# Final normalisation stage: nine in-place row buffers, loads issued by SyncE and ScalarE, stores by GpSimd and SyncE

## The chip, the cores and the metric

One Trainium2 chip, one of its cores. The time is device time of one execution in microseconds; a smaller number is better. The engines are TensorE (PE), VectorE (DVE), ScalarE (ACT), GpSimd (POOL) and SyncE (SP). Transfers between the chip's memory (DRAM) and its on-chip buffer (SBUF) run on 16 DMA engines; they are issued from SyncE's, ScalarE's or GpSimd's instruction stream, each into a queue of its own.

## What is computed

One layer of a trunk: modulation, a token mixing part with a convolution and a recurrent branch, then an expert-choice mixture of sixteen experts, for 1024 latent rows and 128 context rows of 1024 values each. The change concerns the last step alone, the final RMSNorm of both row sets:

```
def rmsnorm(x, g):
    xf = x.astype(jnp.float32)
    y = xf * lax.rsqrt(jnp.mean(xf * xf, axis=-1, keepdims=True) + EPS)
    return (y * g.astype(jnp.float32)).astype(x.dtype)
...
    xp, S_ctx = trunk_layer(xp, c_ctx, s_zero, T_p, *shared)
    xs, _ = trunk_layer(xs, c, state_hgrn[:, l], GRID_W, *shared)
    y_prompt = rmsnorm(xp, final_norm)
    y_sample = rmsnorm(xs, final_norm)
```

## The kernel before

The kernel is written with hand-placed semaphores. It runs in stages. Between two stages stands a barrier of all engines, so that no instruction of a stage is issued before all engines have left the one before it. The last but one stage is the experts': its results are added by indirect transfers from GpSimd into the tensor `x1_d` in DRAM, 1152 rows (nine tiles of 128 rows by 1024 float32, 512 KB each; tiles 0 to 7 are the latent rows, tile 8 the context rows). The last stage reads the nine tiles back, normalises them and stores them as outputs. TensorE has no work in it.

In the last stage:

- SyncE issues the load of `FN` (the row `final_norm`, broadcast to 128 partitions, L2152), then the nine loads `XF <- x1_d` (L2156). `XF` has four buffers: from tile 4 on each load waits until VectorE has finished with tile t - 4, by the semaphore `f_out`.
- ScalarE takes the tiles in order: a Square with a row sum (L2164, in the trace with a short instruction that reads the sum), a Ln (L2167) and an Exp (L2170) make the factor 1 / sqrt(mean + EPS) in `RS3`.
- VectorE multiplies the tile by this factor and by `FN` (L2180) into `YF`, which has three buffers: from tile 3 on it waits for the store of tile t - 3 (`y_stored`).
- GpSimd waits for each result and issues its store (L2187), and at the end waits for all nine.

What sets the order is the order of the tiles in each of the four instruction streams, and the two pools of buffers. The names in the trace leave numbers out: `x_d` is `x1_d`, `out_dram` the output tensors, `RS` is `RS3`, `XJ` the unused squares.

Of the kernel before, what the change touches and what calls it, by code (L numbers as in the profile page):

```python
# [8 lines left out]
ACT = mybir.ActivationFunctionType  # L9
# [7 lines left out]
P = 128  # L17
D = 1024
KT = D // P
TL = 8  # L20
TN = TL + 1
# [55 lines left out]
def trunk(nc, x_prompt, x_sample, state, cond, c_ctx, w_ada, b_ada, norm1, w_in, conv_w, conv_b,  # L77
# [3 lines left out]
    with ctx:  # L81
# [6 lines left out]
        def sem(name):  # L88
            stage_sems.append(nc.alloc_semaphore(name))
            return stage_sems[-1]  # L90
# [7 lines left out]
        def scratch(name, shape):  # L98
            return nc.dram_tensor(name, shape, F32, kind="Internal").ap()
# [7 lines left out]
        x1_d = scratch("x1_d", [T, D])  # L107
# [99 lines left out]
        def wload(eng, slot, src, col):  # L207

            eng.dma_start(W_FULL[:, slot, 1], src[:, :, ds(col, P)]).then_inc(weights_in[slot], 16)
# [31 lines left out]
        with nc.Block() as block:  # L241
            @block.sync
            def _(sp):
                sp.dma_start(CR[0:1, :], c_ctx.rearrange("(a n) -> a n", a=1)).then_inc(cond_in, 16)
                sp.dma_start(CR[1:2, :], cond).then_inc(cond_in, 16)
                for d in range(2):
                    sp.dma_start(LBI[8 * d:8 * d + 8], hgrn_lb[d].rearrange("j (c f) -> c j f", f=P)) \
                      .then_inc(lbi_in, 16)
                sp.dma_start(CST[:], consts).then_inc(const_in, 16)
                for i in range(2):  # L250
                    sp.dma_start(AW[:, i], w_ada_v[:, :, i * 512:(i + 1) * 512]).then_inc(ada_in[i], 16)
                sp.dma_start(MODR[:], b_ada[0].partition_broadcast(2)).then_inc(rows_in, 16)
                sp.dma_start(NR[:, 0, :], norm1[0].partition_broadcast(2)).then_inc(rows_in, 16)
                sp.dma_start(NR[:, 1, :], norm2[0].partition_broadcast(2)).then_inc(rows_in, 16)
                for b in range(2, ADA):

                    sp.wait_ge(ada_mm, b - 1)
                    sp.dma_start(AW[:, b % 2], w_ada_v[:, :, b * 512:(b + 1) * 512]).then_inc(ada_in[b % 2], 16)
                    if b == 9:

                        sp.wait_ge(cond_ct, 1)
                        for slot, off in enumerate((ZF, ZB, IV)):
                            wload(sp, slot, w_in_v, off)
                for slot, off in ((3, Q), (4, OG)):
                    wload(sp, slot, w_in_v, off)
                sp.wait_ge(mod_out, 48)
# [1866 lines left out]

        fn = Region(nc, after_w, hi)
        FN = fn("FN", [P, D])
        XF = fn("XF", [P, 4, D])
        YF = fn("YF", [P, 3, D])
        XJ3 = fn("XJ3", [P, D])
        RS3 = fn("RS3", [P, 2, TN])
        fn_in = sem("fn_in")  # L2140
        xf_in = [sem(f"xf_in{i}") for i in range(4)]
        f_sq = sem("f_sq")
        f_ln = sem("f_ln")
        f_rs = sem("f_rs")
        f_out = sem("f_out")
        y_stored = [sem(f"y_stored{i}") for i in range(3)]
        y_rows = [y_sample[0, t * P:(t + 1) * P, :] for t in range(TL)] + [y_prompt[0]]

        with nc.Block() as block:
            @block.sync  # L2150
            def _(sp):
                sp.dma_start(FN[:], final_norm.partition_broadcast(P)).then_inc(fn_in, 16)  # L2152
                for t in range(TN):
                    if t >= 4:
                        sp.wait_ge(f_out, t - 3)
                    sp.dma_start(XF[:, t % 4], x1_d[t * P:(t + 1) * P, :]).then_inc(xf_in[t % 4], 16)  # L2156

            @block.scalar
            def _(act):
                for t in range(TN):  # L2160
                    act.wait_ge(xf_in[t % 4], 16 * (t // 4 + 1))
                    if t:
                        act.wait_ge(f_sq, t)
                    nc.scalar.activation(XJ3[:], XF[:, t % 4], ACT.Square,  # L2164
                                         accum_out=RS3[:, 0, t:t + 1]).then_inc(f_sq, 1)
                    act.wait_ge(f_sq, t + 1)
                    nc.scalar.activation(RS3[:, 0, t:t + 1], RS3[:, 0, t:t + 1], ACT.Ln, bias=EPS,  # L2167
                                         scale=1.0 / D).then_inc(f_ln, 1)
                    act.wait_ge(f_ln, t + 1)
                    nc.scalar.activation(RS3[:, 1, t:t + 1], RS3[:, 0, t:t + 1], ACT.Exp,  # L2170
                                         scale=-0.5).then_inc(f_rs, 1)

            @block.vector
            def _(dve):
                dve.wait_ge(fn_in, 16)
                for t in range(TN):
                    dve.wait_ge(f_rs, t + 1)
                    if t >= 3:
                        dve.wait_ge(y_stored[t % 3], 16 * (t // 3))  # L2179
                    nc.vector.scalar_tensor_tensor(YF[:, t % 3], XF[:, t % 4], RS3[:, 1, t:t + 1], FN[:],  # L2180
                                                   ALU.mult, ALU.mult).then_inc(f_out, 1)

            @block.gpsimd
            def _(pool):
                for t in range(TN):
                    pool.wait_ge(f_out, t + 1)
                    pool.dma_start(y_rows[t], YF[:, t % 3]).then_inc(y_stored[t % 3], 16)  # L2187
                for i in range(3):
                    pool.wait_ge(y_stored[i], 48)


# [24 lines left out]
```

## Time and profile before

| | us |
|---|---|
| median of 3 runs | 2624.31 |
| lowest and highest | 2623.44, 2630.18 |
| the profiled execution, its own time | 2623.36 |
| its span | 2621.6 |
| last stage, first issue to end of the span | 2587.36 to 2621.6 |
| TensorE busy over the span | 2430.2 (93%) |
| VectorE busy | 1024.7 (39%) |
| ScalarE busy | 841.9 (32%) |
| GpSimd busy | 368.8 (14%) |

The span is what the profiler saw of the execution, from its first to its last event; the execution's own time is a little longer. The shares are averages over all stages, and most of the span is matrix work; the last stage, some 34 us at its end, is read from its own window. Issuing a transfer isn't counted as busy time of an engine; a "q" behind an engine's name means its instruction queue.

### The profile page before, as it was taken

What the parts mean: (1) busy time and instruction counts of PE and PEld (TensorE: products, weight loads), DVE (VectorE), ACT (ScalarE), POOL (GpSimd) and SP (SyncE); (2) the same over time, 40 slices, a digit from 0 to 9 for tenths busy, and PEclk for the clock granted to TensorE, in tenths of its full rate; (3) what the DMA queues carried; (4) which work ended last, traced back from release to release, by engine and by line L of the source; (5) the groups of instructions that cost most, each with busy time, mean ns of one, the idle gap of its engine ahead of it and who ended that gap; (6) DMA issues with size and microseconds to landing.
All of it is one profiled execution on the core that took longest, in us unless ns stands there. A gap on an engine that the chain in (4) does not pass through costs nothing. (4 is left out here: it accounts for less than half of the span.)

```text
span 2621.6 us, 47354 instructions
## 1 busy us (share of the span) xinstructions
PE 2430.2 (93%) x17645; PEld 2293.1 (87%) x17645; DVE 1024.7 (39%) x2630; ACT 841.9 (32%) x1989; POOL 368.8 (14%) x611
## 2 busy tenths in 40 slices
PE   7799999999999999999979989749999999999992
PEld 2399999999999999999979988549999999999992
DVE  2455364545446363545522434642122222222222
ACT  2454444444454444445422012101112111211112
POOL 0011110202111021111111114201010011101011
PEclk9899999999999999999989999879999999999996
DMA  7512112021211112121163433738887887788754
GB/s 268 173 43 62 51 51 62 27 80 35 77 35 55 59 43 72 30 77 43 60 217 101 133 104 121 264 106 267 292 265 242 275 292 253 239 290 283 242 187 161
DMA packets 368217, 376.22 MB, mean 144 GB/s; under 512 B 11803, under 2 KB 340539, under 8 KB 368096
## 3 DMA queue, kind: packets, MB, share of 16 engines
q1 hardware_dynamic: 353928, 326.58, 37.1%
q0 software_dynamic: 14160, 47.81, 6.6%
q8 instruction: 102, 1.67, 0.3%
q14 instruction: 17, 0.14, 0.0%
q10 hardware_dynamic: 10, 0.02, 0.0%
HBM read 330.82 MB, written 43.55 MB: 143 GB/s over the span
## 5 line engine op out<-in xcount | busy, mean ns | idle before, releaser
L717 PE MATMUL bank<-HT,W 128*128 128x384 f32 x5760 | 1049.3, 338 | 27.8 <-issue 15.7
L717 PEld LDWEIGHTS bank<-HT,W 128*128 128x128 f32 x5760 | 995.6, 188 | 33.1 <-issue 30.1
L2016 PE MATMUL bank<-XET,WEA 128*128 128x144 f32 x4096 | 510.9, 287 | 0.6 <-DVE XET L2088 0.6
L2016 PEld LDWEIGHTS bank<-XET,WEA 128*128 128x128 f32 x4096 | 505.5, 191 | 1.3 <-issue 0.7
L2031 PE MATMUL bank<-HID,WED 128*128 128x144 f32 x2048 | 257.8, 287 | 0.0
L2031 PEld LDWEIGHTS bank<-HID,WED 128*128 128x128 f32 x2048 | 252.6, 190 | 0.7
L1409 PE MATMUL bank<-YO,W 128*128 128x384 f32 x960 | 172.0, 336 | 18.5 <-ACT YO L1425 18.5
L1409 PEld LDWEIGHTS bank<-YO,W 128*128 128x128 f32 x960 | 168.3, 189 | 18.8 <-issue 18.8
L2047 ACT ACTIVATE SG<-bank 128x144 f32<-128x144 f32 x128 | 37.3, 291 | 409.5 <-PE bank L2016 409.5
L2117 DVE TENSOR_TENSOR GU<-SG,bank 128x144 f32<-128x144 f32 x128 | 38.9, 304 | 300.4 <-ACT SG L2051 300.4
L2055 ACT ACTIVATE YT<-bank 128x144 f32<-128x144 f32 x128 | 37.3, 291 | 274.3 <-PE bank L2031 274.3
L2099 DVE SCALAR_TENSOR_TENSOR YS<-bank,TW,G 128x512 f32<-128x512 f32 x32 | 24.0, 751 | 254.8 <-PE bank L1993 254.8
L1046 DVE TENSOR_TENSOR W<-W_FULL,W 128x1024 fp32r<-128x1024 f32 x80 | 98.6, 1232 | 32.5 <-ACT W L853 32.4
L1294 POOL TENSOR_TENSOR KH<-X 128x256 f32<-128x256 f32 x32 | 26.4, 835 | 574.2 <-DVE X L1061 387.5
L1935 POOL DMA_INDIRECT x_d<-YS,IDX x16 | 31.3, 1959 | 408.4 <-DVE YC L2099 408.4
L1053 DVE TENSOR_SCALAR KK<-ZS,CWP 128x384 f32<-128x384 f32 x48 | 23.0, 480 | 166.5 <-ACT ZS L868 166.5
L853 ACT ACTIVATE W<-W_FULL 128x1024 fp32r<-128x1024 f32 x80 | 83.7, 1046 | 0.0
L325 PE MATMUL bank<-AW,CT 128*2 128x512 f32 x160 | 73.9, 619 | 6.7 <-DMA AW<-in_w_ada_dram 6.6
L1161 DVE TENSOR_SCALAR ON<-bank,RST 128x128 f32<-128x128 f32 x72 | 25.2, 350 | 128.8 <-ACT RST L980 128.8
L623 POOL TENSOR_TENSOR G<-X 128x128 f32<-128x128 f32 x72 | 35.6, 495 | 270.5 <-PE bank L767 270.5
L2123 DVE TENSOR_TENSOR HID<-GU,bank 128x144 f32<-128x144 f32 x128 | 39.0, 304 | 88.7 <-PE bank L2016 88.7
L949 ACT ACTIVATE QR<-bank 128x384 f32<-128x384 f32 x48 | 23.6, 492 | 143.9 <-PE bank L717 143.9
(218 smaller groups left out, 2794.3 us busy)
## 6 DMA issues: line engine op xcount, KB each, us to landing
WEA<-in_w_e_gate_dram SPq DMA_DIRECT2D x64, 1024.0 KB, 4.8
WEA<-in_w_e_up_dram SPq DMA_DIRECT2D x64, 1024.0 KB, 10.5
WED<-in_w_e_down_dram SPq DMA_DIRECT2D x64, 1024.0 KB, 9.7
W_FULL<-in_w_in_dram SPq DMA_DIRECT2D x80, 512.0 KB, 3.7
AW<-in_w_ada_dram SPq DMA_DIRECT2D x10, 2048.0 KB, 9.0
sg_d<-QR SPq DMA_DIRECT2D x48, 192.0 KB, 1.9
GL<-sg_d POOLq DMA_DIRECT2D x48, 192.0 KB, 2.7
ya_d<-CY SPq DMA_DIRECT2D x24, 192.0 KB, 1.9
```

The lines of the kernel that those rows point to most:

```text
L325: ins = nc.tensor.matmul(PS[1 + b % 2][0:2, :], CT[:, k, :], AW[:, b % 2, k, :], start=(k == 0), stop=(k == KT - 1))
L623: vec.tensor_tensor(o, a, b, ALU.subtract)
L717: ins = nc.tensor.matmul(bank[:, 0:CH], W[:, slot, a, k, :], HT[:, b, k, at * CH:(at + 1) * CH], start=(i == 0 and k == 0), stop=(i == 2 a ...
L853: nc.scalar.activation(W[:, slot, 0], W_FULL[:, slot, 1], ACT.Copy).then_inc(w_hi, 1)
L1046: nc.vector.tensor_tensor(W[:, slot, 1], W_FULL[:, slot, 1], W[:, slot, 0].bitcast(F32), ALU.subtract).then_inc(w_lo, 1)
L1409: ins = nc.tensor.matmul(PS[j % 4][:, 0:CH], W[:, m, a, k, :], src[:, k, n * CH:(n + 1) * CH], start=(i == 0 and k == 0), stop=(i == 2 and ...
L2016: ins = nc.tensor.matmul(PS[2 * s + f % 2][:, 0:NX], WEA[:, 4 * s + f // 2, k, (f % 2) * P:(f % 2 + 1) * P], XET[:, k, :], start=(k == 0), ...
L2031: ins = nc.tensor.matmul(PS[f % 4][:, 0:NX], WED[:, f // 2, k, (f % 2) * P:(f % 2 + 1) * P], HID[:, k, :], start=(k == 0), stop=(k == KT - 1))
L2047: nc.scalar.activation(b, PS[f % 2][:, 0:NX], ACT.Exp, scale=-1.0).then_inc(g_exp, 1)
L2055: nc.scalar.activation(YT[:, f // 4, f % 4], PS[f % 4][:, 0:NX], ACT.Copy).then_inc(yt_made, 1)
L2117: nc.vector.tensor_tensor(GU[:, f % 2], SG[:, f % 2], PS[f % 2][:, 0:NX], ALU.mult) \
L2123: nc.vector.tensor_tensor(HID[:, f], GU[:, f % 2], PS[2 + f % 2][:, 0:NX], ALU.mult) \
```

## The change

The last stage gets a buffer for each of the nine tiles, and VectorE writes its result over the tile that it reads, so that `YF` is gone and no load or result waits for a buffer. The loads are shared: SyncE issues FN and then tiles 1, 3, 5 and 7, ScalarE issues tiles 0, 2, 4, 6 and 8 ahead of its first computation. The stores are shared too: GpSimd issues those of the even tiles, SyncE those of the odd ones, behind its loads. Each load has a semaphore of its own, each storing engine one semaphore for its stores.

```
-        XF = fn("XF", [P, 4, D])
-        YF = fn("YF", [P, 3, D])
+        XF = fn("XF", [P, TN, D])
...
                 sp.dma_start(FN[:], final_norm.partition_broadcast(P)).then_inc(fn_in, 16)
-                for t in range(TN):
-                    if t >= 4:
-                        sp.wait_ge(f_out, t - 3)
-                    sp.dma_start(XF[:, t % 4], x1_d[t * P:(t + 1) * P, :]).then_inc(xf_in[t % 4], 16)
+                for t in range(1, TN, 2):
+                    sp.dma_start(XF[:, t], x1_d[t * P:(t + 1) * P, :]).then_inc(xf_in[t], 16)
+                for t in range(1, TN, 2):
+                    sp.wait_ge(f_out, t + 1)
+                    sp.dma_start(y_rows[t], XF[:, t]).then_inc(y_stored[1], 16)
+                sp.wait_ge(y_stored[1], 64)
...
             @block.scalar
             def _(act):
+                for t in range(0, TN, 2):
+                    act.dma_start(XF[:, t], x1_d[t * P:(t + 1) * P, :]).then_inc(xf_in[t], 16)
                 for t in range(TN):
-                    act.wait_ge(xf_in[t % 4], 16 * (t // 4 + 1))
+                    act.wait_ge(xf_in[t], 16)
...
                     dve.wait_ge(f_rs, t + 1)
-                    if t >= 3:
-                        dve.wait_ge(y_stored[t % 3], 16 * (t // 3))
-                    nc.vector.scalar_tensor_tensor(YF[:, t % 3], XF[:, t % 4], RS3[:, 1, t:t + 1], FN[:],
+                    nc.vector.scalar_tensor_tensor(XF[:, t], XF[:, t], RS3[:, 1, t:t + 1], FN[:],
                                                    ALU.mult, ALU.mult).then_inc(f_out, 1)
...
-                for t in range(TN):
+                for t in range(0, TN, 2):
                     pool.wait_ge(f_out, t + 1)
-                    pool.dma_start(y_rows[t], YF[:, t % 3]).then_inc(y_stored[t % 3], 16)
-                for i in range(3):
-                    pool.wait_ge(y_stored[i], 48)
+                    pool.dma_start(y_rows[t], XF[:, t]).then_inc(y_stored[0], 16)
+                pool.wait_ge(y_stored[0], 80)
```

SyncE's instructions at the end of the program, as a difference (the branches are the ends and beginnings of the stages' code; x9 stands for nine of a kind):

```order
 L1908 COMPARE_AND_BRANCH
 L1901 UNCONDITIONAL_BRANCH
-L2150 UNCONDITIONAL_BRANCH
-L2152 DMA FN<-in_final_norm_dram 128x1024
-L2156 DMA XF<-x_d 128x1024 x9
 L2149 UNCONDITIONAL_BRANCH
+L2151 DMA FN<-in_final_norm_dram 128x1024
+L2153 DMA XF<-x_d 128x1024 x4
+L2156 DMA out_dram<-XF 128x1024 x4
+L2148 UNCONDITIONAL_BRANCH
```

Five of nine loads have left SyncE's stream, and four stores have come in behind the rest.

ScalarE's instructions at the start of the last stage in the changed kernel, up to the end of its first tile:

```order
 L2041 COMPARE_AND_BRANCH
 L1901 UNCONDITIONAL_BRANCH
...
+L2159 UNCONDITIONAL_BRANCH
+L2162 DMA XF<-x_d 128x1024 x5
+L2167 ACTIVATE XJ_7168,RS_7169<-XF 128x1024
+L2170 ACTIVATE RS_7169<-RS_7169 128x1
+L2173 ACTIVATE RS_7169<-RS_7169 128x1
```

The five issues stand ahead of the first tile's three computations; those and all later ones are as before.

GpSimd's instructions at the end of the program, as a difference:

```order
 L1901 UNCONDITIONAL_BRANCH
 L94 ISA
-L2183 UNCONDITIONAL_BRANCH
-L2187 DMA out_dram<-YF 128x1024 x9
-L2149 UNCONDITIONAL_BRANCH
+L2184 UNCONDITIONAL_BRANCH
+L2188 DMA out_dram<-XF 128x1024 x5
+L2148 UNCONDITIONAL_BRANCH
```

Four of nine stores have left GpSimd's stream.

## Rows read from the trace of the kernel before

**Rows 1.** Chain that ended last, 2587 us on: start us, us, what.

```profile
2587.76 5.54 DMA XF<-x_d
...
2598.08 8.01 DMA out_dram<-YF
...
2606.18 1.29 DVE YF L2180
...
2607.49 6.67 DMA XF<-x_d
...
2617.41 0.53 POOL out_dram L2187
```

**Rows 2.** Waits of the last stage: total us, times, longest us.

```profile
ACT XJ L2164 <- DMA XF<-x_d: 30.6, 6, 22.3
DVE YF L2180 <- DMA out_dram<-YF: 9.9, 4, 3.1
...
SPq L2156 <- DVE YF L2180: 16.4, 5, 6.6
```

**Rows 3.** Stretches: length, PE, PEld, DVE, ACT, POOL busy, PEclk, DMA share, GB/s.

```profile
2588.50:2620.00 31.50, 0.00 (x0) 0.00 (x0) 11.56 (x9) 13.66 (x36) 4.91 (x9) 0.50 0.86 317
2588.50:2591.00 2.50, 0.00 (x0) 0.00 (x0) 0.00 (x0) 0.00 (x0) 0.00 (x0) 0.50 0.60 221
2591.00:2595.50 4.50, 0.00 (x0) 0.00 (x0) 0.45 (x1) 2.11 (x5) 0.00 (x0) 0.50 1.02 414
2595.50:2597.00 1.50, 0.00 (x0) 0.00 (x0) 1.35 (x2) 1.44 (x5) 0.35 (x1) 0.50 0.34 137
2597.00:2599.00 2.00, 0.00 (x0) 0.00 (x0) 1.78 (x2) 1.93 (x6) 0.84 (x2) 0.50 0.86 129
2599.00:2603.50 4.50, 0.00 (x0) 0.00 (x0) 1.56 (x2) 2.00 (x7) 0.53 (x1) 0.50 0.96 369
2603.50:2608.50 5.00, 0.00 (x0) 0.00 (x0) 2.19 (x2) 3.06 (x8) 1.06 (x2) 0.50 1.03 419
2608.50:2611.00 2.50, 0.00 (x0) 0.00 (x0) 1.30 (x2) 1.55 (x4) 0.53 (x1) 0.50 0.96 200
2611.00:2614.50 3.50, 0.00 (x0) 0.00 (x0) 0.43 (x2) 0.32 (x1) 0.53 (x1) 0.50 0.99 404
2614.50:2617.00 2.50, 0.00 (x0) 0.00 (x0) 2.38 (x2) 1.24 (x4) 0.53 (x1) 0.50 0.37 151
2617.00:2620.00 3.00, 0.00 (x0) 0.00 (x0) 0.12 (x1) 0.00 (x0) 0.53 (x1) 0.50 0.85 350
2620.00:2621.60 1.60, 0.00 (x0) 0.00 (x0) 0.00 (x0) 0.00 (x0) 0.00 (x0) 0.50 0.00 0
...
2592.00:2592.50 0.50, 0.00 (x0) 0.00 (x0) 0.00 (x0) 0.00 (x0) 0.00 (x0) 0.50 1.06 434
```

**Rows 4.** DMA queues, 2587 us on: packets, MB, share of 16 engines.

```profile
q1 hardware_dynamic: 1440, 5.24, 45.0%
q0 software_dynamic: 1296, 4.72, 33.3%
```

**Rows 5.** Timeline: the first issue of the last stage.

```profile
2587.36 0.35 SPq L2152 DMA_DIRECT2D FN<-in_final_norm_dram  x1
```

**Rows 6.** Timeline: first and fourth tile on ScalarE; groups by line: VectorE's.

```profile
2593.33 1.06 ACT L2164 ACTIVATE XJ<-XF 128x1024 f32<-128x1024 f32 x1 [22.31 <-DMA XF<-x_d]
...
2597.86 1.04 ACT L2164 ACTIVATE XJ<-XF 128x1024 f32<-128x1024 f32 x1
...
L2180 DVE SCALAR_TENSOR_TENSOR YF<-XF,RS,FN 128x1024 f32<-128x1024 f32 x9 | 11.6, 1284 | 32.3 <-ACT RS L2170 22.0 <-DMA out_dram<-YF 9.9
```

**Rows 7.** Timeline of the first stage: two issues by ScalarE, one by SyncE.

```profile
0.90 0.56 ACTq L271 DMA_DIRECT2D CWR<-in_conv_w_dram  x1
1.49 0.23 ACTq L272 DMA_DIRECT2D CWR<-in_conv_b_dram  x1
...
4.18 5.12 SPq L252 DMA_DIRECT2D MODR<-in_b_ada_dram  x1
```

## What the change should do to the time

> **What bounds the kernel now.** The edit touches only the last stage, so I first asked where that stage begins and what ends it. The chain of waits over its window [rows 1] shows no matrix work: from 2587.76 us it runs from a load of 5.54 us through ScalarE and VectorE into a store of 8.01 us, from there through one VectorE operation of 1.29 us into a load of 6.67 us, and from that load through ScalarE and VectorE to the last store. Three transfers take 20.2 of the 33.8 us. The two joints are buffers: VectorE may not write tile 4 until the store of tile 1 has emptied its YF buffer, and SyncE may not load tile 8 until VectorE has finished with an XF buffer. The list of waits says the same in totals: VectorE stood 9.9 us behind stores, SyncE's queue 16.4 us behind VectorE, ScalarE 30.6 us behind loads, of which 22.3 are the start of the stage [rows 2].
>
> Next I asked whether the transfers are slow by themselves. The stretches of the stage [rows 3] give the bytes per second in each. The whole, 2588.5 to 2620.0, moves 31.5 x 317 = 9.99 MB, and the two queues say 5.24 + 4.72 = 9.96 MB [rows 4]. Where both queues have work in hand (2603.5 to 2608.5) the rate is 419 GB/s. At that rate the bytes need 23.8 us, so 31.5 - 23.8 = 7.7 us are lost somewhere. Each stretch loses its length times (1 - rate / 419): 1.2 us in 2588.5 to 2591, 0.05 in the next, 1.0 in 2595.5 to 2597, 1.4 in 2597 to 2599, 0.5 in 2599 to 2603.5, nothing in the next, 1.3 in 2608.5 to 2611, 0.1, then 1.6 in 2614.5 to 2617 and 0.5 in 2617 to 2620; together 7.7. Behind the last byte stand 1.6 us in which nothing moves [rows 3], and before the first 1.1 us from the issue at 2587.36 [rows 5]. Both stay.
>
> **What the engines need.** ScalarE takes a tile every (2597.86 - 2593.33) / 3 = 1.51 us when its loads are there, VectorE 1.28 us [rows 6]. Nine tiles are 13.6 us on ScalarE and 1.3 more on VectorE for the last. From a start at 2593.33, which is where the first load let it begin, VectorE would be done at 2608.2, and the last store would be issued 0.3 later. That is before the 2588.5 + 23.8 = 2612.3 at which the transfers can be through at best. So with buffers for all tiles the stage is bound by its bytes, and my sum is about which of the 7.7 us of lost transfer time come back.
>
> **The change part by part.** The loads: nine buffers instead of four, so none of the five waits in SyncE's queue is left, and every load is in a queue within the first 2 us. *The gap 2595.5 to 2599* (2.4 us) was a queue that had run dry after four tiles, and then a load that started anew. With nine loads in hand the dry part, 1.0 us, surely goes. The slow restart, 1.4 us at 129 GB/s, goes too if it is a restart, and stays if it is the reading of that tile. I take that it goes, since the first four tiles ran at 414 GB/s from the same tensor behind one another: 2.4 back, at the least 1.0.
>
> *The stretch 2608.5 to 2611* (1.3 us at 200 GB/s) is less clear: tile 8 had been asked for at 2607.49 [rows 1], and stores were in hand too, yet the rate fell by half. Either it is again a load started behind a drained queue (gone now) or reads and stores getting in each other's way (it stays or grows). Bounds 0 and 1.3, and I take the middle, 0.65. The 0.5 and 0.1 us of the mixed stretches I leave lost.
>
> *The tail.* From 2614.5 the transfers ran dry because tile 8's load had only just landed: ScalarE, VectorE and the store's issue follow it in series [rows 1]. In the changed kernel, tile 8 leaves VectorE near 2608.2, and then some 1.7 MB of stores are still to be moved (4.1 us at 419), so its own latency is covered. 1.6 + 0.5 = 2.1 us come back, as long as the load of tile 8 has landed in time. From its landing to the end there were 2621.6 - 2614.16 = 7.4 us; for the end that I forecast, 2621.6 - 5.75 = 2615.85, it has to land by 2608.4. Until the first store can move (some 2597) the loads have 8.5 us, which is 3.0 MB of their 5.24 if FN stays slow and 3.5 if not. If they get half of the rate while stores share it, the other 1.7 to 2.2 MB take 8 to 10.5 us (2605 to 2607.5); with two of three queues' shares, 6 to 8 us (2603 to 2605). So it should be in time, with little room, and at the low end I let 0.5 of the 2.1 be lost.
>
> *ScalarE issues five loads.* Its other issues in this program took 0.56 and 0.23 us [rows 7]; five by these are 1.2 to 2.8 us, from about 2587.4 to 2590.2 at the latest, and it has nothing to do before 2592. They lie under the first load, cost 0. Even an issue that is held up, as SyncE's of 5.12 us in the first stage [rows 7], would end by 2593. What this buys: tile 0 is no longer behind FN in one queue. The stretch 2588.5 to 2591 is FN, one row read 128 times, at 221 GB/s, that is 1.2 us lost. If tile 0's packets fill the holes, up to 1.2 come back; if the broadcast holds up the engines themselves, nothing. No row shows two load queues, so I take half, 0.6.
>
> A rule of the Trainium skill speaks against this piece: "DMA: Bandwidth & Descriptors", section "Rules for kernel authors", says that spreading transfers over SyncE, ScalarE and GpSimd brings no bandwidth, since all share the same 16 engines, and saves only issue time. By it the 0.6 are 0 and the gain is 5.15 in place of 5.75. The trace bears it out as far as it goes: one queue alone runs at 414 GB/s, two at 419 [rows 3].
>
> *The stores.* Five by GpSimd (0.53 us an issue [rows 1]) and four by SyncE; three waits of VectorE and the buffers behind them go, 9.9 us of VectorE's idle time in all, but only the parts counted above are on the path. SyncE's stores of tiles 1, 3, 5, 7 stand in its queue behind its own loads of tiles 1 to 7 and wait for VectorE; nothing else is issued behind them. The issue time of a store is hidden as long as stores are in backlog. No bytes are added or taken away; writing in place takes the same three operands of VectorE, cost 0.
>
> **The sum.** 2.4 + 0.65 + 2.1 + 0.6 = 5.75 us. The profiled run took 2623.36 us, 1.76 of it outside its span, and would be 2617.6; the median of the runs shown is 0.95 above that run, so the forecast is 2624.31 - 5.75 = **2618.6 us**, 0.22% less. At the low end 1.0 + 0 + 1.6 + 0 = 2.6 us come back (2621.7), at the high end all 7.7 (2616.6).
>
> The same page's specifications give about 358 GB/s for HBM per core. By that figure, as an estimate, the bytes need 27.9 us and the stage gains 3.6. The trace differs: 419 GB/s over 5 us [rows 3].
>
> **The rivals.** (1) *Reads stay slow beside stores, the gain is small.* For it: the stretch 2608.5 to 2611, and 369 GB/s in 2599 to 2603.5. Against: 419 in 2603.5 to 2608.5 with the same mixture. Two such stretches more than I keep, 1.3 us each, and the slow restart of 1.4 us staying leave 5.75 - 2.6 - 1.4 = 1.75 us: 2622.6. (2) *Slower than before.* If every store that starts beside reads costs such a stretch, 1.3 us for each of nine, 11.7 are added to a best case of 7.7 gained: 4.0 slower, 2628.3. It decides from six stores on (6 x 1.3 = 7.8), and nothing shows it for more than two of the nine. (3) *Everything comes back and the rate is above 419*, since two load queues and two store queues leave no hole: the bytes at 434 GB/s, which one half microsecond reached [rows 3], need 22.9 us, 8.6 gained, 2615.7. Against: no longer stretch is above 419. (4) *The change doesn't do what it says*: if the nine loads can't all be in hand because a queue holds up the issue, as for 5.12 us in the first stage [rows 7], the loads still arrive at the rate of the transfers, and it costs at most the dry 1.0: 2619.6, hardly to be told from the forecast.
>
> **How the numbers follow.** Forecast with its bounds, 2616.5 to 2621.7, and rival 4 with it: 0.72. Rival 1, 2621.7 to 2625: 0.10. Rival 3, gains over 7.9 us: 0.13. Slower than 2625, rival 2 in whole or in part: 0.05, of which 0.03 over 0.3%. A change of 0.3%, 7.9 us, is about the least that a measurement of this kernel can tell from none. So faster by more than that is 0.13, slower 0.03, and 0.84 lie within. The range leaves out half of rival 3 and the far side of rivals 1 and 2: 2615.7 to 2623.5.
>
> **What would show it.** In the changed kernel's profile: the last byte moves near 2614 and the span ends near 2615.8; the rate from 2589 to the end has no stretch under 300 GB/s but the first; VectorE waits for no store; VectorE's last operation ends before 2610, with four stores still on the way. If tile 8's load lands after 2607, the tail has come back. If the stretch of the first 2.5 us stays at 221 GB/s, the 0.6 are gone. The forecast is wrong if the rate falls to 200 whenever stores and loads mix, or if the time moves by more than 8 us, since then something besides this stage's transfers has changed.

## The result, and the profile after

The changed kernel takes 2619.8 us in the median of 20 runs, the kernel before 2624.4 in the median of 20: a ratio of 0.9982 with a 95% interval of 0.9975 to 0.9989, that is 4.6 us less, between 2.9 and 6.6. The forecast was 2618.6 us, 5.75 us less, inside a range of 2615.7 to 2623.5. The interval leaves out a ratio of 1, so the kernel is faster, but by less than the 0.3% that the prediction took as the least that can be told well from none; a change inside that bound was thought most likely.

The last stage, where all of the edit is, shows more than the whole does. Its length, from the first issue to the end of the span, fell from 34.24 us (2587.36 to 2621.6) to 28.03 us. The timeline of the changed kernel at the start of the stage and at its end (start us, us, engine, line, operation):

```profile
2586.57 0.35 SPq L2151 DMA_DIRECT2D FN<-in_final_norm_dram  x1
2586.59 2.89 ACTq L2162 DMA_DIRECT2D XF<-x_d  x5
2586.98 2.26 SPq L2153 DMA_DIRECT2D XF<-x_d  x4
2592.22 1.06 ACT L2167 ACTIVATE XJ<-XF 128x1024 f32<-128x1024 f32 x1 [21.76 <-DMA XF<-x_d]
...
2606.78 1.28 DVE L2181 SCALAR_TENSOR_TENSOR XF<-XF,RS,FN 128x1024 f32<-128x1024 f32 x1 [0.23 <-ACT RS L2173]
2608.35 0.53 POOL L2188 DMA_DIRECT2D out_dram<-XF  x1 [2.48 <-DVE XF L2181]
```

All nine loads are issued within 2.9 us. VectorE's last operation ends at 2608.1, and the span at 2614.6, so the stage runs on for 6.5 us behind it, with stores in all but its last 1.6 us; before, VectorE ended at 2617.1 and the end came 4.5 us later. The waits of the stage in the changed kernel (total us, times, longest), to be held against [rows 2]:

```profile
POOL out_dram L2188 <- DVE XF L2181: 29.3, 5, 18.8
DVE XF L2181 <- ACT RS L2173: 23.8, 9, 21.3
ACT XJ L2167 <- DMA XF<-x_d: 22.5, 2, 21.8
```

VectorE waits for no store any more (9.9 us before), and ScalarE waits for a load twice in place of six times, both at the start. The stretches of the changed kernel (length, busy time of PE, PEld, DVE, ACT, POOL, granted clock, share of the DMA engines, GB/s), which answer to [rows 3]:

```profile
2587.50:2613.00 25.50, 0.00 (x0) 0.00 (x0) 11.56 (x9) 13.23 (x36) 2.79 (x5) 0.50 1.01 391
2587.50:2591.00 3.50, 0.00 (x0) 0.00 (x0) 0.00 (x0) 0.00 (x0) 0.00 (x0) 0.50 0.96 256
2591.00:2596.50 5.50, 0.00 (x0) 0.00 (x0) 1.57 (x2) 3.43 (x9) 0.62 (x1) 0.50 1.01 413
2596.50:2599.00 2.50, 0.00 (x0) 0.00 (x0) 2.28 (x2) 2.38 (x8) 0.00 (x0) 0.50 1.02 419
2599.00:2601.00 2.00, 0.00 (x0) 0.00 (x0) 1.55 (x3) 1.94 (x6) 0.57 (x1) 0.50 1.02 397
2601.00:2612.50 11.50, 0.00 (x0) 0.00 (x0) 6.16 (x5) 5.49 (x16) 1.59 (x3) 0.50 1.03 420
2613.00:2614.60 1.60, 0.00 (x0) 0.00 (x0) 0.00 (x0) 0.00 (x0) 0.00 (x0) 0.50 0.01 3
```

The same 9.97 MB go in 25.5 us instead of 31.5. Against 419 GB/s 1.7 us are lost (25.5 x (1 - 391 / 419)) where 7.7 were, and 1.4 of them lie in one place, the first 3.5 us (3.5 x (1 - 256 / 419)). From there to 2612.5, half a microsecond before the last byte, the engines run at 397 to 420 GB/s.

Why does the whole gain less than the stage? The experiments had both kernels traced a second time. The stage took 34.08 and 28.22 us there, so the pairs agree within 0.2 us, and the change is worth 34.16 - 28.12 = 6.0 us in it. That lies inside the interval of the whole, near its upper end. What scatters is the part ahead of the stage, which is the same code in both kernels. The first 300 us of the kernel before, of its second trace and of run e7 below:

```profile
0.00:300.00 300.00, 265.73 (x1539) 200.19 (x1540) 133.96 (x324) 128.78 (x277) 38.04 (x84) 0.97 0.37 127
```

```profile
0.00:300.00 300.00, 264.49 (x1516) 198.88 (x1517) 129.82 (x314) 126.14 (x272) 38.04 (x84) 0.95 0.38 126
```

```profile
0.00:300.00 300.00, 265.37 (x1498) 197.38 (x1499) 129.12 (x312) 123.53 (x266) 37.04 (x80) 0.94 0.37 125
```

The granted clock of TensorE there, a mean over the 300 us, is 0.97, 0.95 and 0.94, and in the same 300 us 1539, 1516 and 1498 matrix instructions are done. The last stage then begins at 2587.4, 2591.4 and 2596.6 us. This is several times the differences that are to be explained, and so the experiments are read by the length of the stage in their traces. The two traces of one kernel differed by 0.2 us in it. Each experiment below has a single trace, so a few tenths of a microsecond between two of them show nothing.

### The profile page after: what moved, and what is told of

It reads as the page before. It is cut to its first block and busy times, and to the rows that moved or that the text cites. A ratio compares the mean times of both kernels' runs of the same rounds, so it can differ in the third digit from the quotient of the medians.

```text
span 2614.6 us, 47348 instructions
## 1 busy us (share of the span) xinstructions
PE 2430.8 (93%) x17645; PEld 2293.9 (88%) x17645; DVE 1025.1 (39%) x2630; ACT 840.9 (32%) x1989; POOL 366.5 (14%) x607
## 6 DMA issues: line engine op xcount, KB each, us to landing
WEA<-in_w_e_up_dram SPq DMA_DIRECT2D x64, 1024.0 KB, 10.5
```

## The experiments

The stage's length in each trace (us from the first issue to the end of the span):

| kernel | stage |
|---|---|
| before, two traces | 34.24, 34.08 |
| the change, two traces | 28.03, 28.22 |
| e1: nine in-place buffers, loads by SyncE, stores by GpSimd | 28.90 |
| e2b: shared queues, four and three buffers | 31.95 |
| e3: nine load buffers, three result buffers | 30.92 |
| e4: four load buffers, nine result buffers | 31.86 |
| e5: before, tiles 4 to 8 read the rows of 0 to 3 and 0 | 33.61 |
| e6: the change, FN from 128 different rows | 27.99 |
| e7: the change, FN loaded in the experts' stage | 27.13 |
| e8: the change, loads by ScalarE, stores by SyncE | 27.97 |
| e10: e1 with FN loaded in the experts' stage | 27.43 |
| e11: the change, no store before the last loads | 29.81 |

The theory was that the nine buffers bring the gain, since they keep the transfer engines in work, and that the queues bring none. The rival was that the second load queue and the second store queue carry part of it.

### e1: the buffers alone

```
-                for t in range(1, TN, 2):
+                for t in range(TN):
                     sp.dma_start(XF[:, t], x1_d[t * P:(t + 1) * P, :]).then_inc(xf_in[t], 16)
...
-                for t in range(0, TN, 2):
-                    act.dma_start(XF[:, t], x1_d[t * P:(t + 1) * P, :]).then_inc(xf_in[t], 16)
...
-                for t in range(0, TN, 2):
+                for t in range(TN):
                     pool.wait_ge(f_out, t + 1)
                     pool.dma_start(y_rows[t], XF[:, t]).then_inc(y_stored[0], 16)
```

> The nine in-place buffers alone: all loads issued by SyncE, all stores by GpSimd, as before the change. The length of the last stage, from its first issue to the end of the span, was 34.2 us before and 28.0 with the whole change. Theory A (the buffers are the whole gain, all queues share the same engines): 27.8 to 28.8 us, ScalarE's first tile within 1 us of where it was, no stretch after the first 3 us under 380 GB/s. Theory B (the second load queue and the second store queue carry part of it): 29.5 us or more, with stretches under 350 GB/s after the first store.

Its stage took 28.90 us: 5.3 of the 6.0 us are there with one load queue and one store queue, just beyond the window of theory A and clear of theory B. The sign in the rates went the other way: theory A expected no stretch under 380 GB/s behind the start, and there is one under 350, as theory B had it. The whole kernel was at a ratio of 0.9968 (0.9957 to 0.998), 8.9 us less in the medians; 5.3 us is the edge of that interval, and the rest fits the scatter ahead of the stage (its trace enters the last stage at 2585.0 us, the earliest of all). The interval overlaps the change's (0.9975 to 0.9989), so this doesn't show that e1 beats the change; no measurement of the whole kernel shows either that the shared queues are worth having on top of the buffers. The stretches of e1 show most of what the last 0.8 us are:

```profile
2586.00:2589.50 3.50, 0.00 (x0) 0.00 (x0) 0.00 (x0) 0.00 (x0) 0.00 (x0) 0.50 0.97 282
2589.50:2595.50 6.00, 0.00 (x0) 0.00 (x0) 2.77 (x3) 4.69 (x13) 0.74 (x2) 0.50 1.02 416
2595.50:2598.00 2.50, 0.00 (x0) 0.00 (x0) 2.28 (x2) 2.40 (x7) 0.98 (x2) 0.50 0.99 320
2598.00:2611.50 13.50, 0.00 (x0) 0.00 (x0) 6.50 (x6) 6.13 (x18) 3.20 (x6) 0.50 1.01 414
```

One slow stretch, 320 GB/s for 2.5 us, costs 0.6 us; it begins 1.6 us after the first store's issue at 2593.94. All of the 0.80 MB that move in it belong to the load queue: the stores have been issued but move nothing yet. The changed kernel's only dip is 397 GB/s for 2 us, 0.1 us lost, 3.5 us after its first store's issue.

### e2b: the queues alone

```
+                def load(t):
+                    if t >= 4:
+                        sp.wait_ge(f_out, t - 3)
+                    sp.dma_start(XF[:, t % 4], x1_d[t * P:(t + 1) * P, :]).then_inc(xf_in[t % 4], 16)
+                load(1)
+                load(3)
+                for t in range(1, TN, 2):
+                    sp.wait_ge(f_out, t + 1)
+                    if t + 4 < TN:
+                        load(t + 4)
+                    sp.dma_start(y_rows[t], YF[:, t % 3]).then_inc(y_stored[t], 16)
...
+                load(0)
+                load(2)
                 for t in range(TN):
+                    if t in (2, 4, 6):
+                        load(t + 2)
```

> The queues alone: four load buffers and three result buffers as before, but even loads by ScalarE and odd ones by SyncE, even stores by GpSimd and odd ones by SyncE, each still waiting for its buffer. Theory A (the buffers are the gain): the waits stay, the stage keeps 33 to 35 us (before: 34.2), VectorE still waits about 10 us for stores. Theory B (the queues carry part of it): 32 us or less. Since SyncE's stores skip GpSimd's slow first store, some 1 us less than before is possible under A too.

31.95 us, 2.2 less than before: inside theory B's window, at its edge, and outside theory A's. So sharing the queues is worth something while buffers are short. In its trace the dry stretch and a slow one stand as before, but the one at tile 8 is gone:

```profile
2596.00:2598.00 2.00, 0.00 (x0) 0.00 (x0) 1.02 (x2) 1.70 (x5) 0.62 (x1) 0.50 0.19 78
2598.00:2600.00 2.00, 0.00 (x0) 0.00 (x0) 1.43 (x2) 1.94 (x5) 0.00 (x0) 0.50 1.00 344
2600.00:2603.00 3.00, 0.00 (x0) 0.00 (x0) 1.84 (x2) 2.18 (x8) 0.57 (x1) 0.50 1.03 268
2603.00:2614.00 11.00, 0.00 (x0) 0.00 (x0) 4.70 (x4) 6.28 (x17) 1.06 (x2) 0.50 1.02 410
```

VectorE waited 7.5 us for stores (9.9 and 10.3 in the two traces of before). A likely reading is that half of the stores no longer stand in line behind one another in one queue, so buffers come free a little sooner, and the loads that wait for them are issued sooner. It isn't shown: e2b shares the loads and the stores at once, and no run shares only one of them. The two parts alone gave 5.3 and 2.2 us, together 6.0: they mend the same losses, and with all buffers there the shared queues are left with 0.8 us. Even that isn't owed to two queues of each kind, since e8 below has one queue for all loads and one for all stores and is as short as the change (27.97 us).

### e3 and e4: which buffers

```
-        XF = fn("XF", [P, 4, D])
+        XF = fn("XF", [P, TN, D])
```

> Nine load buffers, three result buffers, loads by SyncE, stores by GpSimd. Theory A (a transfer queue that never runs dry is all that counts): VectorE still waits for stores, some 5 to 10 us in all, but the load queue is full until about 17 us into the stage and stores are in hand behind it, so the stage takes 28 to 29.5 us. Rival (VectorE's wait for stores is itself on the path): 31 us or more.

30.92 us, between the theory's 29.5 and the rival's 31, and close to the rival: VectorE's waits for stores are in part on the path. It waited 6.9 us for them, as thought, 5.7 at one time. The stores behind the loads did not stay in hand: from 2608 to 2618.5, with all reads done, the engines ran at 314 GB/s with at most three results on their way:

```profile
DVE YF L2178 <- DMA out_dram<-YF: 6.9, 3, 5.7
```

```profile
2602.50:2608.00 5.50, 0.00 (x0) 0.00 (x0) 1.28 (x1) 4.63 (x14) 0.00 (x0) 0.50 1.01 414
2608.00:2618.50 10.50, 0.00 (x0) 0.00 (x0) 6.38 (x5) 1.32 (x4) 3.20 (x6) 0.50 0.77 314
```

10.5 x (1 - 314 / 419) = 2.6 us are lost there. e1, which differs from e3 only in that results need no buffer of their own, is 2.0 us shorter. e4 has it the other way round:

```
-        YF = fn("YF", [P, 3, D])
+        YF = fn("YF", [P, TN, D])
...
-                    if t >= 3:
-                        dve.wait_ge(y_stored[t % 3], 16 * (t // 3))
```

> Four load buffers, nine result buffers, loads by SyncE, stores by GpSimd: VectorE never waits for a store, but loads from tile 4 on wait for VectorE. Theory A: the dry stretch after the first four tiles stays (1.0 us and 1.4 us of slow start), the rest runs near 400 GB/s: 30 to 31 us. Rival (the result buffers were the main brake): 28.5 us or less. Other rival (the load buffers were): 33 us or more.

31.86 us, beyond the theory's 31. The dry stretch and the slow one behind it are there, 2.0 us lost together (2.4 before), and then comes another 4.5 us at 328 GB/s (1.0 us) that I had not counted:

```profile
2595.50:2597.00 1.50, 0.00 (x0) 0.00 (x0) 1.35 (x2) 1.44 (x6) 0.62 (x1) 0.50 0.22 90
2597.00:2599.00 2.00, 0.00 (x0) 0.00 (x0) 1.74 (x2) 1.87 (x8) 0.57 (x1) 0.50 0.96 242
2599.00:2603.50 4.50, 0.00 (x0) 0.00 (x0) 2.57 (x2) 1.71 (x6) 1.41 (x3) 0.50 0.97 328
2603.50:2615.00 11.50, 0.00 (x0) 0.00 (x0) 5.14 (x4) 6.21 (x16) 1.78 (x4) 0.50 1.02 415
```

Against before (34.16 us, the mean of two traces) load buffers alone bring 3.2 us, result buffers alone 2.3, both 5.3 (e1, where result and load share a buffer). Neither pool was the brake by itself.

### e5: a new start, or a new place?

```
-                    sp.dma_start(XF[:, t % 4], x1_d[t * P:(t + 1) * P, :]).then_inc(xf_in[t % 4], 16)
+                    sp.dma_start(XF[:, t % 4], x1_d[(t % 4) * P:(t % 4 + 1) * P, :]).then_inc(xf_in[t % 4], 16)
```

> The kernel before, but the loads of tiles 4 to 8 read the rows of tiles 0 to 3 and 0 again (the outputs of tiles 4 to 8 are therefore not the reference's). It asks why the load after a pause ran at 129 GB/s (2 us) and tile 8's at 200 GB/s (2.5 us). Theory restart (it is the new start of a load behind a drained queue): both slow stretches stay, each costing 1 us or more, stage 33.5 to 35 us. Theory place (it is the reading of rows not touched for long, a new 2 MB piece at tile 4 and at tile 8): both go, stage 31 to 32.5 us.

33.61 us, and both slow stretches are there although from tile 4 on no load reads a row for the first time:

```profile
2596.00:2597.50 1.50, 0.00 (x0) 0.00 (x0) 1.35 (x2) 1.44 (x5) 0.42 (x1) 0.50 0.35 142
2597.50:2599.50 2.00, 0.00 (x0) 0.00 (x0) 1.78 (x2) 1.90 (x7) 0.77 (x2) 0.50 0.81 205
...
2609.50:2611.50 2.00, 0.00 (x0) 0.00 (x0) 1.73 (x2) 1.17 (x3) 0.15 (x1) 0.50 0.88 250
```

So the place of the rows isn't the cause. The stretches were somewhat milder (1.0 and 0.8 us lost, against 1.4 and 1.3), the second short of the 1 us that the theory asked for; one trace is no proof either way. A new start behind a drained queue fits both, and the changed kernel, which reads tiles 4 and 8 without a pause, shows neither. The start of the stage in e7 below, where FN isn't loaded and no store is issued yet, looks alike: the transfer engines are busy (share 1.03) and move little.

```profile
2597.50:2598.50 1.00, 0.00 (x0) 0.00 (x0) 0.00 (x0) 0.00 (x0) 0.00 (x0) 0.50 1.03 143
```

No run lets a drained queue start anew with nothing else changed, so this stays the reading that fits best.

### e6, e7 and e10: the slow first stretch

```
-                sp.dma_start(FN[:], final_norm.partition_broadcast(P)).then_inc(fn_in, 16)
+                sp.dma_start(FN[:], h2_d[0:P, :]).then_inc(fn_in, 16)
```

> The changed kernel, but FN is loaded from 128 different rows of the scratch tensor h2_d instead of one row 128 times (the outputs are therefore not the reference's). It asks what makes the first 3.5 us of the stage slow, 270 GB/s in place of 419. Theory broadcast (128 reads of one row hold up the engines): the first 3.5 us run at 380 GB/s or more, ScalarE starts 1 us or more earlier, and the stage takes 26.8 us or less (28.0 with the change). Theory start (the first reads of a stage are slow whatever they read): 250 to 300 GB/s as before and a stage of 27.7 to 28.3.

```profile
2590.50:2599.00 8.50, 0.00 (x0) 0.00 (x0) 2.66 (x3) 4.68 (x13) 0.62 (x1) 0.50 1.02 414
2599.00:2603.50 4.50, 0.00 (x0) 0.00 (x0) 3.83 (x4) 4.31 (x13) 0.57 (x1) 0.50 1.01 363
```

The start bears out the broadcast: with 128 different rows the transfers reach 414 GB/s from 2.1 us after the first issue on, where the change needs 4.4 us, and ScalarE begins at 5.0 us instead of 5.65 and 5.73 (0.7 earlier, where the theory asked for 1 or more). The end does not: the stage is 27.99 us, no shorter than the change's. What was won at the start is gone again in a stretch that begins 2.3 us after the first store, 4.5 us at 363 GB/s (0.6 us), six times the loss that the changed kernel had there. So the cost of FN's slow reading is real where it stands, but taking it away did not shorten the stage. It is also less than the 1.4 us lost in the change's first stretch: over the first 4.43 us from the first issue the change moves 202 and 203 GB/s in its two traces and e6 251, which is 0.22 MB, or 0.5 us at 419 GB/s. The rest is lost with 128 different rows too.

e7 issues FN's load in the experts' stage, into a place of its own at the end of the buffer memory:

```
+        FN = nc.alloc_sbuf_tensor_at("FN", [P, D], F32, offset=hi - D * 4)
...
                     sp.dma_start(G2[:, c], mod_d[c, 3].partition_broadcast(P)).then_inc(g2_in, 16)
+                sp.dma_start(FN[:], final_norm.partition_broadcast(P)).then_inc(fn_in, 16)
```

> The changed kernel, with FN loaded in the experts' stage into a place of its own, long before it is used. Both theories of the slow first stretch take away FN's 0.52 MB, 1.25 us at 419 GB/s. Theory broadcast: a further 1.2 us comes back, stage 25.3 to 25.9 us (28.0 with the change). Theory start: 26.5 to 27 us. The whole kernel should be 2 to 2.5 us or 1 to 1.5 us faster than the changed one, some 6.5 or 5.5 us faster than the kernel before.

27.13 us, 1.0 less than the change and above both windows, and e10, the same edit on e1, 27.43, 1.5 less than e1:

> FN loaded in the experts' stage, nine in-place buffers, all loads by SyncE and all stores by GpSimd. Beside the same with FN in the last stage (28.9 us) and beside FN earlier with shared queues (27.1 us). If the queues do nothing, this is 26.5 to 27.5 us, some 2 us less than with FN, of which 1.25 are its bytes; if the shared queues are worth the 0.8 us by which 28.9 and 28.1 differ, it is 27.7 to 28.2 us.

Both are about FN's bytes (1.25 us). e7 again has a slow stretch behind its first store:

```profile
2598.50:2606.50 8.00, 0.00 (x0) 0.00 (x0) 2.92 (x3) 4.82 (x13) 0.62 (x1) 0.50 1.01 414
2606.50:2610.00 3.50, 0.00 (x0) 0.00 (x0) 3.06 (x3) 3.37 (x10) 0.57 (x1) 0.50 0.95 301
```

e10's 27.43 lies in the window for "the queues do nothing", 0.3 us from e7. Its trace shows something that none of the theories has: one microsecond at 250 GB/s, from 4.0 us into the stage, 1.9 us before the first store is issued at 2598.87, with all nine loads in one queue and that queue alone at work.

```profile
2595.97:2596.97 1.00, 0.00 (x0) 0.00 (x0) 0.00 (x0) 0.94 (x4) 0.00 (x0) 0.50 0.96 250
```

A second slow stretch, 310 GB/s from 2600.5 to 2603, begins 1.6 us after the first store's issue, as in e1. As whole kernels e7 and the change are the same: on one chip and beside one another they took 2620.5 and 2620.6 us in the median of 12 runs each, both at a ratio of 0.998 (0.997 to 0.999 for e7, 0.9972 to 0.9989 for the change). The expectation for the change's second measurement:

> The changed kernel once more, beside the one above on the same chip, to see how much of the 6.2 us by which its last stage was shorter in the first trace is there again: stage 27.5 to 28.5 us, whole kernel 4.5 to 6.2 us faster than before. If the stage is again 6 us shorter and the whole only 4.5, something before the last stage costs 1 to 2 us or the runs scatter by as much.

4.6 us less than before, as in the first 20 runs, with a stage of 28.22 us. One more microsecond in the stage is below what this measurement shows, so the gain that was expected of e7 as a whole kernel, 1 us or more over the change, wasn't seen.

### e8 and e11: what makes transfers slow behind the first store

e8 takes GpSimd out of the stage: loads by ScalarE, FN and stores by SyncE.

```
-                for t in range(0, TN, 2):
+                for t in range(TN):
                     act.dma_start(XF[:, t], x1_d[t * P:(t + 1) * P, :]).then_inc(xf_in[t], 16)
...
-                for t in range(1, TN, 2):
+                for t in range(TN):
                     sp.wait_ge(f_out, t + 1)
                     sp.dma_start(y_rows[t], XF[:, t]).then_inc(y_stored[1], 16)
```

> The changed kernel with another split: all nine loads issued by ScalarE, FN and all nine stores by SyncE, none by GpSimd. In the runs so far reads fell to 250 to 340 GB/s for some 3 us, beginning 1 to 2 us after the first store was issued and before the first store's data moved, and GpSimd's first store took about 4 us from issue to its first data. Theory C (what GpSimd does for its first store of the stage disturbs the reads): no such stretch, all stretches after the first 3.5 us of the stage at 380 GB/s or more, a first store that moves data 1 us after its issue, stage 27.0 to 27.6 us. Theory D (writes to the output beside reads do it, whoever issues them): the stretch is there again, right with the first store's data, stage 27.8 to 28.8 us.

```profile
2594.38 13.76 SPq L2154 DMA_DIRECT2D out_dram<-XF  x9
```

```profile
2590.00:2597.00 7.00, 0.00 (x0) 0.00 (x0) 3.56 (x3) 5.47 (x14) 0.00 (x0) 0.50 1.02 414
2597.00:2599.00 2.00, 0.00 (x0) 0.00 (x0) 1.58 (x2) 1.87 (x8) 0.00 (x0) 0.50 1.01 322
2599.00:2612.00 13.00, 0.00 (x0) 0.00 (x0) 6.42 (x5) 5.99 (x16) 0.00 (x0) 0.50 1.02 419
```

The slow stretch is there, 2.6 us after SyncE's first store is issued, and the stage is 27.97 us. Theory C falls: the stretch comes without GpSimd, so GpSimd isn't needed for it. The stage is as short as the change's although all loads go through one queue and all stores through another. e1, 0.9 us longer, differs from e8 in three things: FN goes through the loads' queue, GpSimd issues the stores, and SyncE and not ScalarE issues the loads. No run tells which of them costs the 0.9 us. e11 holds all stores back until the loads of tiles 7 and 8 have landed:

```
+                sp.wait_ge(xf_in[TL - 1], 16)
+                sp.wait_ge(xf_in[TL], 16)
                 for t in range(1, TN, 2):
                     sp.wait_ge(f_out, t + 1)
...
+                pool.wait_ge(xf_in[TL - 1], 16)
+                pool.wait_ge(xf_in[TL], 16)
                 for t in range(0, TN, 2):
                     pool.wait_ge(f_out, t + 1)
```

> The changed kernel, but no store is issued before the loads of tiles 7 and 8 have landed, so that reads never meet a store. With stores in between, reads slowed down 2 to 3 us after the first store's issue, whoever issued it (GpSimd or SyncE), by 0.1 to 0.7 us in all. Theory D (the first stores beside reads do it): the loads run at 400 GB/s or more from 3.6 us after the stage's start to their end, some 15 us after it. Theory T (it comes at that time of the stage or in the middle of the loads, stores or not): a stretch under 370 GB/s at 10 to 14 us is there all the same. The stage itself should take 28 to 30 us, since the turn from loads to stores may leave the engines idle for 1 to 2 us.

```profile
2598.00:2608.00 10.00, 0.00 (x0) 0.00 (x0) 5.53 (x5) 7.86 (x21) 0.00 (x0) 0.50 1.02 417
2608.50:2609.50 1.00, 0.00 (x0) 0.00 (x0) 0.78 (x2) 0.94 (x5) 0.00 (x0) 0.50 0.01 4
```

With no store issued the loads run at 417 GB/s through the time at which the other kernels with nine buffers slow down, which is theory D against theory T: the slow stretch hangs on the first stores, and not on the time or the place in the loads. It needn't be their data, since in e1 they moved none while the rate was low. Nor is it the only thing that slows loads: e10 had its 250 GB/s before any store was issued. Keeping the two apart costs more than it saves, 29.81 us, most of it in the turn, where nothing moves for a microsecond. The cause of these dips stays open.

## Why the prediction held, point by point

- *The stage is bound by its bytes once every tile has a buffer*: right. Between 2591 and 2612.5 there is no stretch under 397 GB/s, and VectorE ends 6.5 us before the span.
- *The gap 2595.5 to 2599, 2.4 us*: all came back, and for the reason given as far as the runs show it. e4, which keeps four load buffers, keeps the gap; e5 shows that the slow part is not the reading of tile 4's rows. That it is the new start is what fits, not what a run shows by itself.
- *The stretch 2608.5 to 2611, half of 1.3 us*: all of it came back, so the term was too small by 0.65. The half that I left lost was meant for reads and stores in each other's way. Slow transfers beside stores do exist, behind the first stores, and cost the change 0.1 us. The other mixed stretches, 0.6 us that the sum left lost, came back too but for that 0.1.
- *The tail, 2.1 us*: came back in full. Tile 8's load was in time: ScalarE began its last tile at 2605.14 without a wait for it, well ahead of the 2607 named as the sign.
- *Tile 0 beside FN, 0.6 us*: this step failed. Two load queues did not fill the holes: 256 GB/s over 3.5 us lose 1.4 us, against 1.2 before [rows 3]. Over the first 4.43 us from the first issue the change moves 202 and 203 GB/s in its two traces, before 194 and 228, and e1, with one load queue, 219. The price was misread too: of the loss at the start only some 0.5 us is FN's one row (e6), the rest is lost with 128 different rows too. The rule of the Trainium skill that I had set against this term ("DMA: Bandwidth & Descriptors", "Rules for kernel authors": several issuing engines bring no bandwidth, only issue time) agrees with these rates. With few buffers sharing the queues was worth 2.2 us all the same (e2b), while VectorE's waits for stores fell from 9.9 and 10.3 us to 7.5.
- *ScalarE's five issues*: 2.89 and 2.80 us in the two traces, at or just beyond the bound of 2.8, and hidden: they end at 2589.48, and ScalarE then still waits for tile 0's load until 2592.22. Its first tile starts 5.65 and 5.73 us after the stage's first issue, against 5.97 and 5.55 before, which is no gain.
- The stage came out at 6.0 us less by two pairs of traces, the sum said 5.75: 0.65 and 0.5 too little, 0.6 and 0.2 of the start too much. That the sum is within 0.3 us is partly luck, since these errors nearly cancel; the big terms, 2.4 and 2.1, held by themselves. The whole came out at 4.6 us less (2.9 to 6.6). Whether the missing 1.4 us are scatter or something ahead of the stage could not be settled. Nothing in the traces points to the latter.
- *The rivals*: a slow stretch behind the first stores (1, 2) came once a stage and cost 0.1 to 1.0 us in the kernels with nine buffers, not 1.3 for each store. A gain over 7.9 us (3) would have needed a quick start and more than 419 GB/s throughout; the longest stretch reached 420. The nine loads were all issued within 2.9 us, so no queue held them up (4).

## What to carry to other kernels

Where a stage is made of transfers, add its bytes, divide by the rate of its best stretch, and look for the stretches that lie below it: that gives the most that buffers can bring, and names the places. Here buffers for all tiles mattered more than who issues (5.3 us of 6.0); sharing the queues helped while buffers were scarce (2.2 us) and hardly at all after that. And a gain of 0.2% in one stage is read from the stage's own length in two traces each, since the part ahead of it scattered by up to 11.6 us between traces.

## What the runs showed that was not expected

- While one row is read 128 times in a load of 512 KB, all transfers together run at 256 to 284 GB/s for about 3 us (the change, e1, e8), where 128 different rows let them reach 414 GB/s 2.1 us after the first issue (e6). The difference is about 0.5 us. Taking FN out of the stage shortened it by about its bytes (1.0 and 1.5 us, e7 and e10, against 1.25).
- The first microsecond in which a stage's loads move is slow without FN too: 143 GB/s with the transfer engines busy (e7), 270 in e10.
- With nine buffers the rate of all transfers falls to 301 to 397 GB/s for 2 to 4.5 us, beginning 1.6 to 3.5 us after the first store's issue, whoever issues it; later stores run beside reads at 412 to 420 GB/s. Without stores no such stretch came in e11, but e10 had one of a microsecond at 250 GB/s before its first store.
- Nine loads of 512 KB issued in a row take 4.82 us of their queue (e1), 0.54 each, and five on ScalarE beside four on SyncE 0.58 and 0.57 each (the change).
